# A two-layer hybrid backbone on one core: branch products in the order gating, attention, DeltaNet, and residuals ahead of the next stage's weights

## The reference, cut to what matters

```
h += 1/2 * gate1 * SwiGLU(mod1(RMSNorm(h)))
h += gate2 * W_o( sum_b sigmoid(g_b) * P_b(branch_b(mod2(RMSNorm(h)))) )
h += 1/2 * gate3 * SwiGLU(mod3(RMSNorm(h)))
```

```python
m = (sigmoid(ga) * (ya @ w_a) + sigmoid(gb) * (yb @ w_b) + sigmoid(gc) * (yc @ w_c))
return m @ w_o
```

## Time and profile before

| | |
|---|---|
| median of three runs | 2602.66 us |
| profiled execution | 2605.7 us, its span 2603.9 us, mean granted PE clock 0.967 |
| PE | busy 2477.6 us (95%), 15918 matmuls |
| DVE | busy 1474.4 us (57%) |
| ACT | busy 941.4 us (36%) |
| chain that ended last | PE 88%, DVE 7%, ACT 2%, issue 2%, DMA 1% |
| weight panels `ring<-in_wts` | 288 issues of 1024 KB, 4.8 us to landing (median) |

### The profile page before, as it was taken

One profiled execution on the slowest core, in us unless ns is written; L12 is line 12 of the kernel. 1 busy time (PEld: TensorE's weight loads), 2 busy tenths in 40 slices (PEclk: granted clock), 3 DMA queues, 4 the chain that ended last, 5 costly groups with the idle time before them and its releaser, 6 DMA issues.

```text
span 2603.9 us, 37980 instructions
## 1 busy us (share of the span) xinstructions
PE 2477.6 (95%) x15918; PEld 2106.9 (81%) x15918; DVE 1474.4 (57%) x2299; ACT 941.4 (36%) x1523; POOL 78.2 (3%) x110
## 2 busy tenths in 40 slices
PE   5999999989989999989999999999999989999999
PEld 3888877857878878878888778888886778899999
DVE  5877655255657364567754553333354667566555
ACT  2322223355543322232222132222244554444543
POOL 0000000000023000000000000000000003100000
PEclk8999999999999899989999989999989999999999
DMA  6554542201200033325555422222321220045454
GB/s 267 208 187 177 185 155 95 75 33 49 82 34 2 33 145 114 130 82 196 191 189 183 148 105 97 98 97 97 113 97 66 82 81 3 15 163 179 149 189 166
DMA packets 44665, 309.67 MB, mean 119 GB/s; under 512 B 5073, under 2 KB 6225, under 8 KB 7633
## 3 DMA queue, kind: packets, MB, share of 16 engines
q1 hardware_dynamic: 44208, 305.98, 32.4%
q10 hardware_dynamic: 288, 1.27, 0.1%
HBM read 306.18 MB, written 1.05 MB: 118 GB/s over the span
## 4 chain that ended last, share of the span: by engine, by line
PE 88%; DVE 7%; ACT 2%; issue 2%; DMA 1%; POOL 0%; SPq 0%; ACTq 0%; DVEq 0%
PE bank L1412 72%; PE bank L1765 6%; PE bank L1405 2%; PE bank L1710 1%; PE bank L1689 1%; DVE w_lo L2010 1%; DVE u_lo L2057 1%; ACT w_hi L893 1%; DVE sq L2049 1%; PE bank L1455 1%; PE bank L1443 1%; PE bank L1698 1%; PE bank L1625 1%; DVE work L2474 1%; DMA mod_par<-in_mod 0%
## 5 line engine op out<-in xcount | busy, mean ns | idle before, releaser
L2010 DVE TENSOR_TENSOR w_lo<-ring,w_hi 128x1024 fp32r<-128x1024 f32 x420 | 511.2, 1224 | 761.8 <-ACT w_hi L893 756.9
L1412 PE MATMUL bank<-u_hi,w_hi 128*128 128x512 f32 (+1 forms) x2272 | 821.7, 362 | 27.6 <-DVE w_lo L2010 15.9
L1412 PE MATMUL bank<-u_hi,w_lo 128*128 128x512 f32 (+1 forms) x2272 | 813.1, 358 | 0.0
L1412 PE MATMUL bank<-u_lo,w_hi 128*128 128x512 f32 (+1 forms) x2272 | 812.1, 357 | 0.0
L893 ACT ACTIVATE w_hi<-ring 128x1024 fp32r<-128x1024 f32 x420 | 443.3, 1059 | 887.8 <-PE bank L1412 885.7
L1412 PEld LDWEIGHTS bank<-u_hi,w_hi 128*128 128x128 f32 x2272 | 440.1, 194 | 95.5 <-issue 22.5
L1412 PEld LDWEIGHTS bank<-u_lo,w_hi 128*128 128x128 f32 x2272 | 439.5, 193 | 59.9
L1412 PEld LDWEIGHTS bank<-u_hi,w_lo 128*128 128x128 f32 x2272 | 440.3, 194 | 58.2
L1412 PE MATMUL bank<-hidden_hi,w_hi 128*128 128x512 f32 (+1 forms) x722 | 261.3, 362 | 0.0
L1412 PE MATMUL bank<-hidden_lo,w_hi 128*128 128x512 f32 (+1 forms) x722 | 260.7, 361 | 0.0
L1412 PE MATMUL bank<-hidden_hi,w_lo 128*128 128x512 f32 (+1 forms) x722 | 260.6, 361 | 0.0
(11 more groups left out here) (231 smaller groups left out, 2490.8 us busy)
## 6 DMA issues: line engine op xcount, KB each, us to landing
ring<-in_wts SPq DMA_DIRECT2D x288, 1024.0 KB, 4.8
h<-in_x SPq DMA_DIRECT2D x8, 256.0 KB, 4.0
par<-in_par ACTq DMA_DIRECT2D x2, 620.0 KB, 6.0
out<-h SPq DMA_DIRECT2D x8, 128.0 KB, 3.6
cst<-in_cst SPq DMA_DIRECT2D x1, 704.0 KB, 12.0
mod_par<-in_mod SPq DMA_DIRECT2D x1, 96.0 KB, 11.9
cond<-in_c SPq DMA_DIRECT2D x1, 8.0 KB, 1.6
```

Of the source, the lines that this page charges most:

```text
L1412: last = weights.used(pe.matmul(out, lhs[a], rhs[b], start=start and n == 0, stop=stop and n == 2))
L2010: tt(w_lo[:, b % HALVES, :], half_source(n % RING, part), w_hi[:, b % HALVES, :].bitcast(F32), ALU.subtract).then_inc(panel_left[n % RING] ...
```

## The change

Four things change. The branches of the merge are gone through in the order 0, 2, 1 (gating, attention, DeltaNet), on PE and DVE, in the list of who drains which product, and in the weight stream; the gates keep their order. PE waits ahead of each of the three branch halves of the first group for one more low part, instead of for all three ahead of the first. DVE makes the low parts of ya and yc between the second and the third scaling of yb's heads. And DVE prepares the next stage's first panel behind the last residual (its first part) instead of ahead of residual j = 6; if no stage follows nothing changes.

```diff
+BRANCHES = (0, 2, 1)
...
-            for n, b in enumerate(("gm", "dn", "mla")):
+            for n, b in enumerate(("gm", "mla", "dn")):
                 half(rows(inp["w_branch_" + b][l], cols))
...
-                    for kind, who in (("gate", "a"), ("branch", "v")):
-                        for b in range(3):
+                    for kind, who, order in (("gate", "a", range(3)), ("branch", "v", BRANCHES)):
+                        for b in order:
...
-                    for b in range(3):
+                    for n, b in enumerate(BRANCHES):
                         w2 = weights.half(UNIT)
                         if gq == 0:
-
-                            pe.wait_ge(y_rest_ready, 3 * (l + 1))
+                            pe.wait_ge(y_rest_ready, 3 * l + n + 1)
...
                     g, c = divmod(j, 2)
-                    splits.past((l, "down", f), 6 * g + 4 + c)
+
+                    if following is None or j < DC - 2:
+                        splits.past((l, "down", f), 6 * g + 4 + c)
+                    elif j == DC - 2:
+                        splits.past((l, "down", f), 21)
                     if carry is not None and j == 2:
                         modulations(carry, 7)
                     second = residual((l, "down", f, j), l, 0 if f == 0 else 2, j, w, following)
+                splits.past((l, "down", f), 23)
                 return second
...
                 for i in range(HEADS):
                     dve.wait_ge(outs_spread, HEADS * l + i + 1)
                     stt(yb[:, i, 0:w], yb[:, i, 0:w], par_of("dn_out"), bank[5 + i % 2][:, 0:w], ALU.mult, ALU.mult).then_inc(outs_scaled, 1)
+                    if i == 1:
+                        y_rest(0, ya, 1)
+                        y_rest(2, yc, 2)
...
                 splits.past((l, "merge"), 4)
-                y_rest(0, ya, 1)
-                splits.past((l, "merge"), 5)
-                y_rest(2, yc, 2)
                 y_rest(1, yb, 3)
...
-                    for b in range(3):
-                        splits.past((l, "merge"), h0 + 6 + b)
+                    for n, b in enumerate(BRANCHES):
+                        splits.past((l, "merge"), h0 + 6 + n)
...
                     if j % 2 == 0:
-                        splits.upto(START[l, "out"] + j // 2 + 2)
+                        splits.upto(START[l, "out"] + min(j // 2 + 2, 4))
                     second = residual((l, "out", j), l, 1, j, w, (l, 2))
+                splits.upto(START[l, "out"] + 5)
                 norm(l, 2, second)
```

More of the change, by code:

```diff
@@ L2528, in _, with y_rest @@
                     dve.wait_ge(out_kept[d], outs_before(l, 4, d))
+                def y_rest(b, y, n):
+                    dve.wait_ge(y_rounded, 3 * l + n)
+                    tt(y_lo[b][:, :, 0:w], y[:, :, 0:w], y_hi[b][:, :, 0:w].bitcast(F32),
+                       ALU.subtract).then_inc(y_rest_ready, 1)
                 splits.past((l, "merge"), 0)
@@ L2564, in _ @@
                             m = macc[:, c, 0:w]
-                            dst = m if b == 0 else mtmp[:, c, 0:w]
+                            dst = m if n == 0 else mtmp[:, c, 0:w]
                             tt(dst, sig[:, 2 * b + c, 0:w], bank_of(key)[:, 0:w], ALU.mult).then_inc(drained["v"], 1)
-                            if b:
+                            if n:
                                 wait_drained(dve, key)
                                 last = tt(m, m, mtmp[:, c, 0:w], ALU.add)
-                                if b == 1:
+                                if n == 1:
                                     step(last)
```

## The result

| | before | changed |
|---|---|---|
| median of its runs | 2598.67 us (4 runs, 2592.46 to 2602.77) | 2565.98 us (4 runs, 2560.73 to 2571.26) |
| profiled execution | 2605.7 us | 2561.39 us, span 2559.6 us, clock 0.981 |

What follows compares the result with a forecast made beforehand. TensorE (PE) was taken as the bound, busy 2477.6 of 2603.9 us. Waits 17.3, merges' clock 3.75 and borders' clock 3 made 24: 2605.7 to 2581.7, and 2579 as the runs' median lies 3.0 lower; range 2570 to 2590.

Steps and rivals of the forecast that it cites:

- the borders' clock: Lower PE clock after pauses at the five stage borders: 3 us given back, with bounds of -4 and 16.
- E: Last border between stages (2407 us), one-part product: sums 1.35 us earlier, reciprocal held by low halves, 1.2 us saved.
- the merges' clock: First 12 matmuls behind each merge pause run at full spacing: 2.45 us in layer 0, 1.3 in layer 1, 3.75 together.
- A: First border (422 us), a down projection: PE's sums of squares come 2.41 us earlier, the reciprocal's delay hidden.
- B: Second border (1139 us), output projection: PE's wait of 1.58 us at the sums goes and no more.
- C and D: Third and fourth borders (1530 and 1908 us), down projections: 2.41 us of wait each, 4.82 together.
- Four added waits: Two more PE waits per layer at the merge's branches: estimated 0.2 to 0.4 us, but not seen in the trace.
- (a): Rival: borders give nothing, as the two low halves cost the reciprocal what the residual gained; 2592 us, chance 0.10.
- (b): Rival: merge gap returns behind the branches through a late drain or panel 4; 2585 to 2587 us, chance 0.10.
- (e): Rival: DVE's idle stretch moves, so PE waits for ya alone until the same time; about 2598 us, chance 0.03.
- (c): Rival: the clock does not drop at the borders, 13 us more gained; 2567 us, chance 0.07.
- (d): Rival: slower, ACT's DeltaNet gate sigmoid waits for DVE at six places, then PE for ACT; 2609 us, chance 0.03.

Runs made afterwards that it cites:

- r10: Kernel before with unused matmuls filling PE's pauses ahead of the sums and the second pause at each border, waits kept: 2586.81 us, 0.9954.
- r11: Kernel before with 33 and 26 unused matmuls in the pauses ahead of the first branch product of layers 0 and 1, waits kept: 2597.67 us, 0.9987.
- e1: Changed kernel with the residual part undone, so only the merge's part is left: 2582.61 us, 0.9946 against the kernel before.
- e8: Changed kernel with second border pauses filled, e6's edit, and layer 0's second FFN splitting its second panel before the first adaLN panel: 2550.35 us, 0.9812.
- e6: Changed kernel with the one-column sums over yb's heads issued between chunks of the first gate product instead of ahead of it: 2560.0 us, 0.9844.
- r12: The kernel of e8 run again without a further edit: 2556.51 us, 0.9829 against the kernel before.

## Why the prediction was right, and where it was wrong

The account of the real 32 to 34 us, each term from a row or a run: waits 17.7 (4.08 and 3.24 in the merges, 10.6 at the borders' sums less 0.23 at E's reciprocal), the borders' clock 12 (r10), the merges' clock 3.4 (r11). That is 33.1. The 12 are for nearly all of the low clock at the borders; the changed kernel keeps 3.5 to 20 us of it, and the remainder of the residual part alone gives 8. So the sum is good to some 5 us.

- **Waits, 17.3 forecast, 17.7 found.** Both merge waits went whole, with the cover that was counted (1.1 us forecast, 1.22 found). A gave 2.64 where 2.41 were counted, B 1.58 as counted, C and D 2.52 and 2.47 for 2.41 each. At A, C and D the reciprocal behind the two low halves is hidden, as worked out, with a cover of 0.1 us at A. At E 1.39 us of wait went and 0.23 came back at the reciprocal, which makes 1.16 where 1.2 stood; the step had 1.35 and 0.15.
- **The merges' clock, 3.75 forecast, 3.4 measured (none to 7).** The spacing behind the gates is the full one from the first matmul on, so the mechanism stands; the run bounds its size only loosely.
- **Four added waits.** No row shows one: between 912 and 1100 us PE waits for nothing. Across the two new waits of layer 0, near 915.7 and 921.3, the spacing is 0.23 us like that of its neighbours. The Trainium skill (Advanced Engine Details and Errata, Network/Comms) gives 50 to 100 ns for reading a semaphore, from which the prediction made an estimate of 0.2 to 0.4 us; it is not seen here, where the queue is full.
- **The borders' clock: the step that failed.** "One of two pauses stays, so I stay near the lower end and take **3**" was the term, with bounds of -4 and 16. It measured 12 (7 to 16) with both pauses filled, and 8 (3 to 14) as the remainder of the residual part alone. The upper bound was well made, from about 30 matmuls on the path at each border: between the two traces 15.7 us came there. What was wrong was the choice within it. The step took for granted that the pause that stays costs most of the clock as before. In fact the low clock at the borders goes from 41 to 58 us with both pauses as they were to 3.5 to 20 without the first. By the account, this term makes the 9 us between the forecast gain of 24 and the 33 that came.
- **Rivals.** (a), (b) and (e) gave 2592, 2585 to 2587 and 2598; nothing of them is there, save (a)'s mechanism at E with 0.23 us. The sign set for (a), a spread that waits over 0.5 us for the reciprocal, is met at E by the letter (0.78), but 0.55 of it stood there before. (c), the clock does not drop, had 0.07 and is nearly what came: its 2567 lies 1 us from the first median and 3 from the second. That it lies so near is in part luck, since it started from the 2602.66. The clock does hold at four of the five borders of one trace, but at two of the other. (d), ACT waiting for DVE at DeltaNet's sigmoid, does not occur: ACT's sigmoids there wait for PE alone.
- **The range** ended at 2570 because (c) had been given little weight. With a term whose bounds are 20 us apart, the far part of it belonged in.

Open: how far the chip's part of the clock can be set by the order of the work. The experiments show what fewer pauses do to the time on average, not what decides a single execution. No run leaves the first pause of a border and takes the second, so it is not known whether that would give back as much.

## What to carry to other kernels

A wait on TensorE can cost more than its own length when the clock falls behind it: here border waits of 1.6 to 2.75 us, worth 10.4 us by themselves, cost 18.7, and the price of the clock was measured apart by filling the pauses with matmuls that nobody reads. Such a filling run is the experiment to make before a clock term is guessed. Where two pauses stand close together and one of them goes, do not take it for granted that the other keeps the clock down: here taking the first left 3.5 to 20 of 41 to 58 us. Let the range reach to the full bound of the term.

## What the runs showed of the hardware that was not expected

- The granted clock falls in different places in executions of one kernel. The changed kernel's ten runs lie in two groups, 2560.65 to 2561.39 and 2569.39 to 2574.35. Over 40 executions of the kernel before, those beside e1 to e8, the span grows by 0.36 us for each us of low clock (159 us of it on average; 100 in the first trace of the changed kernel). At half the clock a PE that sets the pace throughout would lose 0.5. That another engine sets the pace at some of these places would explain the difference; no run shows it.
- PE can be busy without a gap and yet be at the lower clock: 16 us at 0.50 over a run of one-column matmuls and the first gate product (860 to 876), just behind a pause of 1.59. With the same matmuls between matmuls of 512 columns, and a shorter pause, two of three traces have 1.00 there (e6 and r12, not e8); between matmuls of 256 columns, in layer 1, none of the three has.
- Matmuls that do nothing useful made the kernel before 12 us faster (0.9954 [0.9937, 0.9972]).
